# A hybrid decoder step on one core: the sample tokens' delta states are updated in each head's turn, not in a stage of their own

## The reference, cut to what matters

```
S' = a S + k (beta (v - a S^T k))^T          per sequence and head, S is 128x128
o  = S'^T q / sqrt(128)
o_b = RMSNorm(o) * w * silu(z)               then o_b goes into the mix with branch A
```

## Time and profile before

| what | us |
|---|---|
| median of 3 runs (lowest, highest) | 2618.58 (2617.45, 2620.59) |
| the profiled execution's own time | 2620.2 |
| its span, first to last instruction | 2618.4 |
| PE, DVE, ACT, GpSimd busy | 2346.7, 1070.3, 646.9, 0.2 |

### The profile page before, as it was taken

One profiled execution on the slowest core, in us unless ns is written; L12 is line 12 of the kernel. 1 busy time (PEld: TensorE's weight loads), 2 busy tenths in 40 slices (PEclk: granted clock), 3 DMA queues, 4 the chain that ended last, 5 costly groups with the idle time before them and its releaser, 6 DMA issues. The chain is left out here.

```text
span 2618.4 us, 35138 instructions
## 1 busy us (share of the span) xinstructions
PE 2346.7 (90%) x13864; PEld 2160.8 (83%) x13864; DVE 1070.3 (41%) x1882; ACT 646.9 (25%) x1400; POOL 0.2 (0%) x4
## 2 busy tenths in 40 slices
PE   5888987569999999999997769796999999979898
PEld 3677876459999999999996559675999999968676
DVE  4132221345666665766664633353222222231233
ACT  4123222104233232243341100352111111131211
POOL 0000000000000000000000000000000000000000
PEclk6999988559999999999998579898999999989999
DMA  4010201411121121111201444442222222041432
GB/s 155 9 65 9 82 11 51 139 38 39 44 62 41 44 69 41 44 52 34 69 28 46 147 139 152 155 127 76 70 72 72 72 72 71 25 150 44 138 109 61
DMA packets 224158, 191.38 MB, mean 73 GB/s; under 512 B 30253, under 2 KB 197198, under 8 KB 224047
## 3 DMA queue, kind: packets, MB, share of 16 engines
q1 hardware_dynamic: 212792, 152.71, 20.1%
q10 hardware_dynamic: 11302, 37.82, 3.6%
HBM read 138.57 MB, written 52.11 MB: 73 GB/s over the span
## 5 line engine op out<-in xcount | busy, mean ns | idle before, releaser
L271 PE MATMUL bank<-xT_hi,w_lo 128*128 128x344 f32 x1152 | 391.5, 340 | 3.6 <-DVE w_lo L267 3.6
L273 PE MATMUL bank<-xT_hi,w_hi 128*128 128x344 f32 x1152 | 369.0, 320 | 0.0
L272 PE MATMUL bank<-xT_lo,w_hi 128*128 128x344 f32 x1152 | 368.8, 320 | 0.0
L271 PE MATMUL bank<-xT_hi,ffn_lo 128*128 128x344 f32 x1056 | 338.3, 320 | 12.3 <-DVE ffn_lo L267 12.3
L273 PE MATMUL bank<-xT_hi,ffn_hi 128*128 128x344 f32 x1056 | 337.8, 320 | 0.0
L272 PE MATMUL bank<-xT_lo,ffn_hi 128*128 128x344 f32 x1056 | 337.3, 319 | 0.0
L271 PEld LDWEIGHTS bank<-xT_hi,w_lo 128*128 128x128 f32 x1152 | 218.2, 189 | 3.7 <-issue 3.7
L272 PEld LDWEIGHTS bank<-xT_lo,w_hi 128*128 128x128 f32 x1152 | 218.3, 189 | 0.0
L273 PEld LDWEIGHTS bank<-xT_hi,w_hi 128*128 128x128 f32 x1152 | 217.4, 189 | 0.0
L271 PEld LDWEIGHTS bank<-xT_hi,ffn_lo 128*128 128x128 f32 x1056 | 199.3, 189 | 12.4 <-issue 12.4
L273 PEld LDWEIGHTS bank<-xT_hi,ffn_hi 128*128 128x128 f32 x1056 | 198.9, 188 | 0.0
(11 more groups left out here) (373 smaller groups left out, 4109.0 us busy)
## 6 DMA issues: line engine op xcount, KB each, us to landing
w_raw<-in_w_in SPq DMA_DIRECT2D x48, 512.0 KB, 3.9
ffn_raw<-in_w_ffn_in SPq DMA_DIRECT2D x44, 512.0 KB, 5.0
act_scr<-ffn_y ACTq DMA_DIRECT2D x22, 516.0 KB, 2.6
fo_sr<-act_scr SPq DMA_DIRECT2D x16, 704.0 KB, 6.6
fo_wr<-in_w_ffn_out SPq DMA_DIRECT2D x22, 512.0 KB, 5.2
gate_scr<-gate ACTq DMA_DIRECT2D x16, 516.0 KB, 2.9
a_kv_raw<-in_w_in SPq DMA_DIRECT2D x3, 2048.0 KB
mix_ta<-gate_scr SPq DMA_DIRECT2D x8, 516.0 KB, 4.9
```

Source lines behind the costliest of these rows:

```text
L271: nc.tensor.matmul(out, stat_lo, mov_hi, start=start, stop=False)
L272: nc.tensor.matmul(out, stat_hi, mov_lo, start=False, stop=False)
L273: return nc.tensor.matmul(out, stat_hi, mov_hi, start=False, stop=stop)
```

## The change

The stage `sample_delta_block` and the tile `samp` are gone. Each head's turn now holds the step of its own 8 states:

- GpSimd, which had no part in the heads, has a program: for each head it waits for the store of the head before, loads 8 states (512 KB) into `S0`, multiplies them by the decay, waits for the update (`s_add`) and stores them. Its DMAs are on its own queue.
- PE gets a ones-matmul for the norms (`s_nm`), eight state matmuls with k and q as columns and a ones-matmul for k.q (`s_k`), eight broadcasts of `vn`'s columns by transposes (`s_bc`), and a ones-matmul for the output's norm (`s_rms`), each at a place in the written order.
- DVE gets small ops on 128x8 and eight updates of 128x128, which multiply the broadcast by k and add the state; ACT gets Ln and Exp on 128x16 and 128x8.
- In the last turn only, the convolution's inputs are turned, copied and stored beside the projection's steps 49 to 63, and the outputs of heads 0 to 6 are loaded (into `pre` and `w_raw`, which are free by then) and split at the steps in `OB_STEP`; head 7's output is split from where it lies, without its trip through DRAM.
- `oaT` is split at the start of mix (`prelude`).

The diff, cut (the removed stage is in the listing above; indentation is narrowed):

```diff
-samp = sb(early, "samp", [P, 4, HB, NS])
...
-def sample_delta_block():
...
+def pair_block(name, turns, nk_a, rhs_a, rhs_b, w_a, w_b, gates, out_scr, prelude=None):
...
+    if prelude is not None:
+      pe.wait_ge(a_lo, 1)
...
+      split_weights_hi(act, rhs_a[0][:], prelude).then_inc(a_hi, 1)
...
+      v.wait_ge(a_hi, 1)
+      split_lo(v, rhs_a[1][:], prelude, rhs_a[0][:]).then_inc(a_lo, 1)
...
+S0 = sb(s, "s_state", [P, NS, P])
...
+ob_buf = [pre[m][:, :L] for m in range(3)] + [w_raw[j][:].rearrange("p k c -> p (k c)") for j in range(2)]
+conv_rows = [x[:3 + NS, :D] for x in (*gate, tanh)]
...
+OB_STEP = [66, 74, 82, 90, 98, 106, 114]
...
+  if is_last(h):
+    for r in range(2):
+      yield 49 + 11 * r
+      wt(pe, "cn", HB, 0)
+      for g in range(3):
+        if r == 0:
+          wait(pe, evac[g], HB, 2)
+        else:
+          pe.wait_ge(conv_copied, g + 1)
+        for n in range(4):
+          last = nc.tensor.transpose(banks[g][:3 + NS, n * P:(n + 1) * P],
+                       conv_new[:, 12 * r + 4 * g + n], ident[:])
+        last.then_inc(conv_turned, 1)
...
+    for x in range(HB - 1):
+      yield OB_STEP[x]
+      act.wait_ge(conv_turned, 1)
+      act.wait_ge(ob_ld[x % 5], 16 * (x // 5 + 1))
+      split_weights_hi(act, xT_hi[:, x, :L], ob_buf[x % 5]).then_inc(ob_hi, 1)
...
+    def conv_copy(r):
+      for g in range(3):
+        v.wait_ge(conv_turned, 3 * r + g + 1)
+        n = 3 * r + g
+        nc.vector.tensor_copy(conv_rows[n // 2][:, (n % 2) * 512:(n % 2) * 512 + 512],
+                   banks[g][:3 + NS, :]).then_inc(conv_copied, 1)
+    yield 58
+    v.wait_ge(gout, 16 + HB * 32)
+    conv_copy(0)
+    yield 63
+    conv_copy(1)
+    for x in range(HB - 1):
+      yield OB_STEP[x]
+      v.wait_ge(ob_hi, x + 1)
+      split_lo(v, xT_lo[:, x, :L], ob_buf[x % 5], xT_hi[:, x, :L]).then_inc(ob_lo, 1)
...
+    if n == 2:
+      wt(pe, "s_oln", i, 0)
+    if n == 3:
+      wt(pe, "s_add", i, 0)
...
+  fill.upto(done[0] - 5)
+  wt(pe, "k_ev", i, 2); wt(pe, "s_sq", i, 1)
+  inc(nc.tensor.matmul(banks[4][:, :2 * NS], ident_ones[:], s_sq[:].rearrange("p n u -> p (n u)"),
+            start=True, stop=True), "s_nm")
...
-  wt(pe, "k_ev", i, 2); wt(pe, "q_ev", i, 2); wt(pe, "v_ev", i, 1); wt(pe, "cols", i, 1)
+  wt(pe, "q_ev", i, 2); wt(pe, "v_ev", i, 1); wt(pe, "cols", i, 1); wt(pe, "s_ln", i, 1)
...
+  wt(pe, "samp_m", i, 1); wt(pe, "s_dec", i, 1); wt(pe, "vn", i, NT)
+  for u in range(NS):
+    nc.tensor.matmul(banks[5][:, 2 * u:2 * u + 2], S0[:, u], s_kq[:, u], start=True, stop=True)
+  inc(nc.tensor.matmul(banks[5][:, 2 * NS:3 * NS], ident_ones[:], s_qk[:], start=True, stop=True), "s_k")
+  fill.upto(done[TAIL] - 12)
+  wt(pe, "s_vn", i, 1); wt(pe, "osq", i, NT)
+  for b in range(2):
+    for p in range(4):
+      c = s_vn[:, 4 * b + p:4 * b + p + 1]
+      last = nc.tensor.transpose(banks[6 + b][:, p * P:(p + 1) * P], c.to_broadcast([P, P]), ident[:])
+    inc(last, "s_bc")
+  fill.upto(done[TAIL] - 7)
+  wt(pe, "s_o2", i, 1)
+  inc(nc.tensor.matmul(banks[5][:, 3 * NS:4 * NS], ident_ones[:], s_o2[:], start=True, stop=True), "s_rms")
...
+  wt(act, "s_nm", i, 1)
+  inc(nc.scalar.activation(s_r[:].rearrange("p n u -> p (n u)"), banks[4][:, :2 * NS], ACT.Ln,
+              bias=eps_col[:]), "s_ln")
...
+  wt(act, "s_ln", i, 1)
+  inc(nc.scalar.activation(s_r[:], s_r[:], ACT.Exp, scale=-0.5), "s_r")
...
+  wt(act, "s_rms", i, 1)
+  inc(nc.scalar.activation(s_rms[:], banks[5][:, 3 * NS:4 * NS], ACT.Ln, scale=1.0 / DK,
+              bias=eps_col[:]), "s_oln")
+  wt(act, "s_oln", i, 1)
+  inc(nc.scalar.activation(s_rms[:], s_rms[:], ACT.Exp, scale=-0.5), "s_oln")
   fill.slot(TAIL + 1)
+  if isinstance(i, int):
+    for b in range(2):
+      cs = slice(512 * b, 512 * b + 512)
+      wt(act, "ob", i, b + 1)
+      split_weights_hi(act, xT_hi[:, HB - 1, cs], ob_out[:, cs]).then_inc(ob_hi, 1)
+    wt(act, "s_ob", i, 1)
+    split_weights_hi(act, xT_hi[:, :, L:], ob_s[:]).then_inc(ob_hi, 1)
+    return
...
+  wait(v, silu, i, 2)
+  nc.vector.tensor_tensor(s_sq[:, 0], qc[:, L:], qc[:, L:], ALU.mult)
+  inc(nc.vector.tensor_tensor(s_sq[:, 1], kc[:, L:], kc[:, L:], ALU.mult), "s_sq")
...
-  wait(v, silu, i, 4)
-  for n, x in enumerate((qc, kc, vc, zs)):
-    x = nc.vector.tensor_copy(samp[:, n, bass.ds(i, 1)], x[:, L:].unsqueeze(1))
-  inc(x, "samp_m")
+  wt(v, "s_r", i, 1); wait(v, silu, i, 4)
+  nc.vector.scalar_tensor_tensor(s_kq[:, :, 1], qc[:, L:], DK ** -0.5, s_r[:, 0], ALU.mult, ALU.mult)
+  nc.vector.tensor_tensor(s_vb[:], vc[:, L:], eg_h[1], ALU.mult)
+  inc(nc.vector.tensor_tensor(s_kq[:, :, 0], kc[:, L:], s_r[:, 1], ALU.mult), "s_v")
+  wt(v, "s_v", i, 1)
+  inc(nc.vector.tensor_tensor(s_qk[:], s_kq[:, :, 0], s_kq[:, :, 1], ALU.mult), "samp_m")
...
+  wt(v, "s_k", i, 1)
+  inc(nc.vector.tensor_tensor(s_t[:, 0], by[:, :, 0], eg_h[1], ALU.mult), "s_v")
+  wt(v, "s_v", i, 2)
+  inc(nc.vector.tensor_tensor(s_vn[:], s_vb[:], s_t[:, 0], ALU.subtract), "s_vn")
+  wt(v, "s_vn", i, 1)
+  inc(nc.vector.tensor_tensor(s_t[:, 1], s_vn[:], banks[5][:, 2 * NS:3 * NS], ALU.mult), "s_v")
+  wt(v, "s_v", i, 3)
+  inc(nc.vector.tensor_tensor(s_ov[:], s_t[:, 1], by[:, :, 1], ALU.add), "s_v")
+  wt(v, "s_v", i, 4)
+  inc(nc.vector.tensor_tensor(s_o2[:], s_ov[:], s_ov[:], ALU.mult), "s_o2")
...
+  for b in range(2):
+    wt(v, "s_bc", i, b + 1)
+    for p in range(4):
+      u = 4 * b + p
+      x = nc.vector.scalar_tensor_tensor(S0[:, u], banks[6 + b][:, p * P:(p + 1) * P],
+                       s_kq[:, u, 0:1], S0[:, u], ALU.mult, ALU.add)
+    inc(x, "s_add")
...
+  wt(v, "s_oln", i, 2)
+  nc.vector.tensor_tensor(s_ov[:], s_ov[:], s_rms[:], ALU.mult).then_inc(s_nrm.sem, 1)
+  v.wait_ge(s_nrm.sem, s_nrm.at(i, 1))
+  inc(nc.vector.scalar_tensor_tensor(ob_s[:, bass.ds(i, 1)].rearrange("p o u -> p (o u)"), s_ov[:],
+                   norm_dv[:], zs[:, L:], ALU.mult, ALU.mult), "s_ob")
+  if isinstance(i, int):
+    for b in range(2):
+      cs = slice(512 * b, 512 * b + 512)
+      v.wait_ge(ob_hi, HB + b)
+      split_lo(v, xT_lo[:, HB - 1, cs], ob_out[:, cs], xT_hi[:, HB - 1, cs]).then_inc(ob_lo, 1)
+    v.wait_ge(ob_hi, HB + 2)
+    split_lo(v, xT_lo[:, :, L:], ob_s[:], xT_hi[:, :, L:]).then_inc(ob_lo, 1)
...
+    def ob_load(h):
+      if h < 3:
+        wait(sp, conv, HB, 0); wt(sp, "cn", HB, 0)
+      elif h < 5:
+        wait(sp, wlo[0], HB, 1); wait(sp, wlo[1], HB, 1)
+      else:
+        sp.wait_ge(ob_lo, h - 4)
+      sp.wait_ge(out_dma, 16 + 16 * h + 16)
+      sp.dma_start(ob_buf[h % 5], ob_scr[h, :, :L]).then_inc(ob_ld[h % 5], 16)
+
+    for h in range(3):
+      ob_load(h)
     base_to(sp, HB - 1)
     base_from(sp, HB - 1)
+    sp.dma_start(o["conv_s"][0, :, 0:2], a["state_conv"][0, :, 1:3]).then_inc(conv_out, 16)
+    for h in range(3, 5):
+      ob_load(h)
+    sp.wait_ge(conv_copied, 6)
+    for n, rows in enumerate(conv_rows):
+      cs = slice(D * n, D * n + D)
+      sp.dma_start(o["conv_p"][0, 0, :, cs], rows[:3]).then_inc(conv_out, 16)
+      sp.dma_start(o["conv_s"][0, :, 2, cs], rows[3:]).then_inc(conv_out, 16)
+    for h in range(5, HB - 1):
+      ob_load(h)
+    sp.wait_ge(conv_out, 16 * 7)
...
+  @block.gpsimd
+  def _(pool):
+    for h in range(HB):
+      if h:
+        pool.wait_ge(s_out, 16 * h)
+      pool.dma_start(S0[:], a["state_delta"][0, :, h].rearrange("b k v -> k b v")).then_inc(s_ld, 16)
+      pool.wait_ge(s_ld, 16 * h + 16)
+      inc(nc.gpsimd.tensor_tensor(S0[:], S0[:], eg_s[:, 0, h].unsqueeze(2).to_broadcast([P, NS, P]),
+                    ALU.mult), "s_dec")
+      pool.wait_ge(E["s_add"].sem, E["s_add"].at(h, 2))
+      pool.dma_start(o["delta_s"][0, :, h].rearrange("b k v -> k b v"), S0[:]).then_inc(s_out, 16)
+    pool.wait_ge(s_out, 16 * HB)
...
-sample_delta_block()
...
+   lambda n: wb_v[:, :, bass.ds(n * P, P)], True, mix_scr, oaT[:])
```

More of the change, by code:

```diff
@@ L1225, in pair_block @@
-        def pair_block(name, turns, nk_a, rhs_a, rhs_b, w_a, w_b, gates, out_scr):
+        def pair_block(name, turns, nk_a, rhs_a, rhs_b, w_a, w_b, gates, out_scr, prelude=None):
             nk = nk_a + KT
@@ L1737, in heads_block @@
                       sm=NT + 1, m1=NT, vn=NT, m2=NT, m3=NT, o_ev=NT, osq=NT, oln=2, on=2, ot_tr=2, ob=2,
-                      samp_m=1, cn=3)
-            E = {k: ev(k, n, -1 if k in ("ob", "ssq") else 0) for k, n in D1.items()}
+                      samp_m=1, cn=3, s_sq=1, s_nm=1, s_ln=1, s_r=1, s_v=4, s_k=1, s_vn=1, s_bc=2, s_o2=1, s_rms=1,
+                      s_oln=2, s_ob=1, s_add=2, s_dec=1)
+            E = {k: ev(k, n, -1 if k in ("ob", "ssq", "s_oln", "s_add") else 0) for k, n in D1.items()}
+            s_ld, s_out, s_nrm = sem("s_ld"), sem("s_out"), ev("s_nrm")
+            conv_turned, conv_copied, conv_out = sem("co_tr"), sem("co_cp"), sem("co_out")
+            ob_ld, ob_hi, ob_lo = [sem("ob_ld") for _ in ob_buf], sem("ob_hi"), sem("ob_lo")
             out_dma = sem("ob_out"); st_dma = sem("state_out"); cleared = sem("ub_cleared")
```

(11 more changed lines are left out.)

168 lines of the change are left out of this document (13 added, 155 removed).

## The result

The changed kernel took 2572.43 us in the median of 4 runs (2568.69 to 2575.22), the kernel before 2619.59 (2617.45 to 2622.63) beside it. The ratio is 0.9818 [0.9801, 0.9835], so 47 us less. The forecast was 2573. Run once more with five rounds, it gave 2572.16 and 0.9815 [0.9802, 0.9828]. The profiled execution took 2572.3, with a span of 2570.5 against 2618.4.

A forecast was written before the change was run, and what follows sets the result against it. PE bounds the heads at full clock; in the sample delta stage engines take turns. Terms -84.4 + 23.1 + 2.4 + 13.5 = -45.4 us, so 2574.8 for the profiled execution, 2573 as median; 8-in-10 range 2562 to 2591.

The forecast's parts named there:

- What goes: Stage between heads and mix: its 91.9 us vanish, but 7.1 us of semaphore clearing stays and grows 0.4; net -84.4 us.
- What PE gets: Turns 0 to 6: thirty more PE instructions at 0.11 us each, 3.3 us a turn, 23.1 us for seven.
- GpSimd: All eight turns: store, load and decay hidden, except decay beside DVE's column work; 0.3 us a turn, 2.4 us in all.
- The mechanism that the forecast gave 22%: Rival, 22%: decay holds up DVE's column ops and PE waits, 1.3 us a turn; 2581, or 2590 with the base chain.
- (1): Last turn, inverse's base: DVE's convolution-row copies wait for the gates' store, so PE's base transposes come 4.1 us later.
- (2) and (3): Last turn, inverse: DVE copies and a split before the first level's evacuation, +1.4; a split before the last level's, +1.0.
- (4): Last turn, scan: four splits, each where DVE had 0.64 us of idle, 0.6 us apiece, +2.5 us.
- (5): Last turn, tail: state matmuls, small ops, updates, head 7's splits and a wait for the last states' store, +3 us.
- The last turn at half clock: Rival, 10%: PE at half clock from the inverse's base to the scan's start, +10 us, 2583.
- Unscaled state matmuls: Rival, 7%: state matmuls in turns 0 to 6 don't speed up with the clock, 12 us more, 2585.
- more is covered: Rival, 6%: half of the last turn's additions and GpSimd's 2.4 us vanish, 2564.
- Slower than before: Rival, 3%: DVE stands still while GpSimd multiplies, every turn; decides from 7.0 us per decay; at 8.5 us, 2631.

The follow-up runs named there:

- the run with one matmul: The changed kernel with one state matmul of 16 columns in place of eight with 2 columns each: 2563.58 us, ratio 0.9780.
- the run with earlier additions: The changed kernel with convolution rows in the tiles of q, k and v, and copies and first splits before the inverse's levels in the last turn: 2569.01 us.

## Why the prediction was right

**What goes.** Predicted -84.4 us with the clearing left standing. The stretch from the scan to mix shrank by 82.1, and with the 2.2 us that the tail got in it (below) the term comes out at -84.3. The clearing took 7.6 us for a predicted 7.5.

**What PE gets.** Predicted 3.3 us a turn, measured 3.33 where there is no decay. The step that could have failed was the price of a state matmul, known only from a stretch at half clock. Both ways of reading it were open, and the chosen one (the time scales with the clock) is shown by the 1.84 us for sixteen and by the run with one matmul.

**Waits in these turns.** None but the columns', as argued. Without the decay the turns differ by 0.01 us: DVE's additions, the updates and the base's way through DRAM all stay under the projection.

**GpSimd.** Predicted 0.3 us a turn between 0 and 1.3; measured 0.1 (0 in three or four turns of seven, at most 0.53). The mechanism that the forecast gave 22% is real: it is that rival's, with a smaller price. The margin of 1 us was read rightly. The price was too high in two respects: the decay takes 1.89 us and not 2.3, and it seldom covers the columns whole. Even when forced upon them it costs 0.38 a turn, 2.7 us in all and not 8 to 10.

The Trainium skill (SBUF — State Buffer, Who interferes with whom) had said that GpSimd and a DVE op with two SBUF inputs exclude each other for a whole instruction. The traces agree: the columns end with the decay, and a split beside it takes 2.17 us for 1.22. The 2.2 us that I had estimated from the Trainium skill's GPSIMD Engine Reference (Elementwise — side-by-side cycle accounting) stand against 1.89 measured. What the rule can't tell is the margin, and that decided.

**The last turn.** Predicted +12.0 and +1.5 for the clock, measured +10.7 to the heads' end. Term by term: (1) the gates 5.2 for 4.1, since their store landed 3.7 us after its issue (the forecast had put 3.25: the page's 2.9, which counts from the issue, on top of the issue's 0.35), and the half clock of 1412 to 1420 sits in it; (2) and (3) 1.5 together for 2.4; (4) the scan 1.8 for 2.5, that is 0.45 and not 0.6 a split; (5) the tail 2.2 for 3: from the scan's last state op to the heads' end it is 11.6 us, before 9.4.

**Mix.** Predicted 0, measured 0.4.

**The other rivals.** The last turn at half clock didn't come in the changed kernel: about 7 us at the base, then full through the scan. The run with earlier additions had the half clock in another place, the scan and the tail, where it cost 2.8 and 1.6 us. Unscaled state matmuls fall with the run above. Of "more is covered" there is a little: the terms for waits and for the last turn were all on the high side but one, by 5 to 6 us in sum with the 1.5 for the clock, and the gates were 1.1 on the low side. Slower than before would have needed 7 us of hold per decay; the worst measured is about 1.6 (1.95 instead of 0.4 for the columns). In all the forecast for the profiled execution was -45.4 and it measured -47.9, although the stages that the change doesn't touch took 2.1 us more. So the terms together were 4.6 us too cautious, and that the median (2572.43) came within 1 us of the forecast (2573) is partly luck.

## What to carry to other kernels

Work moved from a stage where engines take turns into a stretch where one engine is full cost here what it added to that engine (3.33 us a turn for thirty instructions), so count its instructions and price them at the clock of the new place. The rest is margins: for each op that lands on another engine, find who waits for it and how long it could have been late; 1.3 us of hold on a margin of about 1 us cost 0.4. And where a tile is borrowed, ask for whose DMA the borrower now waits: picking other tiles for the rows was worth 3.5 us up to the scan by the trace.

## What the runs showed of the hardware that I had not expected

The hold works both ways. In the last turn of the changed kernel a DVE product of two SBUF tiles was under way when the decay began, and now GpSimd's op was the longer one, 2.34 us instead of 1.89:

```profile
1380.83 0.69 DVE L2094 TENSOR_TENSOR kbe<-k_tok 128x512 f32<-128x512 f32 x1
```

```profile
1380.94 2.34 POOL L2288 TENSOR_TENSOR s_state<-s_state,eg_s 128x1024 f32<-128x1024 f32 x1 [4.25 <-DMA s_state<-in_state_delta]
```

A DVE op that reads one input from PSUM isn't held. With the doubled decay, turn 2:

```profile
849.80 0.68 DVE L2103 TENSOR_TENSOR vb<-bank,beta_all 128x512 f32<-128x512 f32 x1
849.87 1.89 POOL L2289 TENSOR_TENSOR s_state<-s_state,eg_s 128x1024 f32<-128x1024 f32 x1 [5.69 <-DMA s_state<-in_state_delta]
```

It took 0.68 us, like all sixteen of its kind in this run, though the decay ran for nearly all of that time. And the granted clock can fall to its half level in the scan and stay there for over 20 us (1444 to 1466), though PE is busy for nearly all of them (the run with earlier additions); the changed kernel kept the full one through its scan.
